# Rows of the decays' running sums spread over the partitions: TensorE products replaced by a DRAM scratch and broadcast loads, in the state-space stage of a hybrid decoder block

## The chip, the cores and the metric

The kernel runs on one NeuronCore of one Trainium2 chip. The metric is the device time of one execution in microseconds; a kernel's time is the median of several executions.

## The reference, cut to what matters

One decoder block on 1024 tokens of width 1024, all in f32: a mixer with two groups of heads (a Mamba-2 state-space group with 8 heads of 64, and a latent attention group), then a mixture of 32 experts. The change is in the state-space group, in chunks of 128 tokens:

```python
    adt = jnp.moveaxis((dt * a).reshape(b, nc, SSD_CHUNK, g, r), 2, -1)
    ...
    a_cs = jnp.cumsum(adt, axis=-1)
    decay = jnp.exp(segsum(adt))     # exp(a_cs[l] - a_cs[s]) for s <= l, else 0
    cb = jnp.einsum('bclgn,bcsgn->bcgls', cc, bc)
    y_diag = jnp.einsum('bcgrls,bcsgrp->bclgrp', cb[:, :, :, None] * decay, xd)
    decay_states = jnp.exp(a_cs[..., -1:] - a_cs)
    states = jnp.einsum('bclgn,bcgrl,bclgrp->bcgrpn', bc, decay_states, xd)
    ...
    y_off = jnp.einsum('bclgn,bcgrpn,bcgrl->bclgrp', cc, prev, jnp.exp(a_cs))
```

For each chunk and head, `decay` is a matrix of 128 x 128. With the source token `s` on the partitions, its argument needs `a_cs[s]`, one number a partition, and `a_cs[l]`, a row of 128 numbers that every partition must hold. That row is what the change is about.

## The kernel before, in words

The program is five blocks, one after the other; at the end of a block all engines meet at a barrier. Block 1 (from L294) makes the conditioning and the input projection, block 2 (L729) the attention, block 3 (L1035) the state-space stage, block 4 (L1287) the output projection and the router, block 5 (L1593) the experts. Inside a block each engine (TensorE or PE, ScalarE or ACT, VectorE or DVE, GpSimd or POOL, and SP, which here only issues DMAs) runs its own list of instructions in the order in which it is written, and waits on semaphores for the others.

Block 3 loops over `NT` = 8 chunks of `P` = 128 tokens. With `H` = 8 heads in `G` = 2 groups, `HG` = 4 heads a group. Ahead of the loop DVE works out `dt_all` and `adt` (L1159 to L1173; in the profile such small tiles are all called `slim`), PE makes `acs` and `tot`, the running sums and totals of all chunks and heads as a [128 x 64] tile each (L1045, L1046), and DVE copies them to SBUF. SP issues one load of 4 MB, `w_out_sb` (L1038), which block 4 reads.

The loop is software-pipelined: on PE and DVE `front(ch + 1)` comes before `back(ch)`.

- PE, `front`: transposes of x (L1058) and B (L1063), the product C B (L1068), and the products of L1076: for each head, `adt` of this head, broadcast over 128 columns, against the triangle `tri`. Its result is the row `a_cs[l]` on every partition, in PSUM banks 3 and 4, one for each group.
- DVE, `front`: `xd` = x dt (L1190), `cb` = C B masked (L1193), then for each group `decay` = row - `acs` (L1198) and its minimum with 0 (L1200), `xsk` (L1201), and, when ACT has taken the exponential (L1138), `decay` times `cb` (L1207).
- PE, `back`: the part from the state (L1087), the new state (L1094), the part inside the chunk (L1103, with `decay` as weights). DVE, `back`: `state` (L1216), `y_part` (L1225, L1227).
- POOL: `xds` (L1251) of the next chunk, `state_d` (L1260), `y_part` + `xsk` (L1265), gating by `zs` (L1267), and from the third chunk on two small steps of an inverse root (L361, L363).

DVE's `xd` of chunk ch waits for `ssd_ysum`, POOL's L1265 of chunk ch - 2. PE's L1058 waits for `ssd_xsk`, DVE's L1201. PE's L1076 waits for `ssd_arg`, DVE's L1200, which frees the banks, and DVE's L1198 waits for PE's L1076:

```python
                    for g in range(G):
                        if ch:
                            pe.wait_ge(S["ssd_arg"], 2 * ch - 1 + g)
                        for j in range(HG):
                            h = g * HG + j
                            last = pe.matmul(BANK[3 + g][:, j * P:(j + 1) * P], adt[:, ch, h:h + 1].to_broadcast([P, P]),
                                             tri[:, :], start=True, stop=True)
                        last.then_inc(S["ssd_rows"], 1)
```

## Time and profile before

| | |
|---|---|
| median of 3 runs | 1243.04 us (1242.4 to 1243.77) |
| the profiled execution, its own time | 1242.94 us |
| its span, first to last instruction | 1240.3 us |
| state-space stage, in the timeline | 516.39 to 603.37 us |
| PE busy | 1061.1 us, 86% of the span |
| DVE busy | 506.4 us, 41% |
| POOL busy | 210.0 us, 17% |

The durations come from that one profiled execution. A time in the timeline is counted from the start of the span. "L1198" is line 1198 of the kernel before; an f32 product is two matmul instructions in the trace, a transpose is one. Where DVE instructions don't wait, the next one starts about 0.08 us before the end of the last that the trace shows.

### The profile page before, as it was taken

The numbers are of one execution on the slowest core, as the hardware profiler recorded it, in microseconds if no ns is written. First come the engines' busy times: TensorE is split into PE (matmuls) and PEld (weight loads), VectorE is DVE, ScalarE is ACT, GpSimd is POOL, SyncE is SP. The second block draws the span as 40 slices with busy tenths as digits, with TensorE's granted clock in tenths as the row PEclk, the third lists the DMA queues.
The fourth block names the chain that finished last, engine by engine and source line by source line (L and its number), as shares of the span: only waits on it lengthen the run. The fifth ranks groups of instructions, "written<-read, shape, count | busy, mean of one in ns | idle before, by whom it ended". The sixth has DMA issues, their size and how long they took to land. (4 is left out here: it accounts for less than half of the span.)

```text
span 1240.3 us, 11686 instructions
## 1 busy us (share of the span) xinstructions
PE 1061.1 (86%) x4040; PEld 591.2 (48%) x4040; DVE 506.4 (41%) x825; ACT 260.0 (21%) x585; POOL 210.0 (17%) x324
## 2 busy tenths in 40 slices
PE   1499999996989999787699994399999999999954
PEld 1444444443455666587345553244445445444521
DVE  4543437345656555588143345511121112112217
ACT  1420001213444344233022211011111111111113
POOL 5100000223200000046210000112221221222114
PEclk9989999997999999898699996599999999999977
DMA  9763332000000000300401216238887878988537
GB/s 334 260 261 136 136 136 42 1 1 0 1 1 1 1 1 1 135 2 1 141 35 68 68 51 241 107 131 344 305 313 307 319 302 322 348 323 320 211 135 290
DMA packets 46355, 190.05 MB, mean 153 GB/s; under 512 B 17314, under 2 KB 18402, under 8 KB 29026
## 3 DMA queue, kind: packets, MB, share of 16 engines
q1 hardware_dynamic: 34596, 166.80, 35.8%
q0 software_dynamic: 10672, 18.45, 4.2%
q10 hardware_dynamic: 1040, 4.19, 0.9%
q8 instruction: 27, 0.44, 0.1%
q14 instruction: 20, 0.16, 0.0%
HBM read 182.07 MB, written 26.21 MB: 168 GB/s over the span
## 5 line engine op out<-in xcount | busy, mean ns | idle before, releaser
L1715 PE MATMUL PS<-w_gu,xg_T 128*128 128x512 f32 x544 | 241.5, 597 | 1.1 <-ACT xg_T L1800 1.1
L1715 PEld LDWEIGHTS PS<-w_gu,xg_T 128*128 128x128 f32 x544 | 101.8, 192 | 116.8 <-issue 115.2
L1726 PE MATMUL PS<-w_dn,hid_T 128*128 128x512 f32 x272 | 122.5, 593 | 0.9 <-DVE hid_T L1878 0.9
L1344 PE MATMUL PS<-w_out_sb,cat_T 128*128 128x512 f32 x256 | 113.5, 602 | 2.8 <-ACT cat_T L1400 2.8
L673 PE MATMUL PS<-hT,w_in_sb 128*128 128x512 f32 x256 | 112.2, 601 | 0.0
L1875 DVE TENSOR_TENSOR hid<-PS,hid_s 128x256 f32<-128x256 f32 x34 | 14.4, 425 | 224.2 <-ACT hid_s L1803 224.2
L361 POOL TENSOR_SCALAR rstd<-stat 128x1 f32<-128x1 f32 (+1 forms) x48 | 21.9, 456 | 408.1 <-ACT junk L468 206.3
L991 PE MATMUL PS<-kT,qT 96*128 96x512 f32 (+4 forms) x192 | 76.6, 509 | 3.0 <-ACT qT L782 3.0
L673 PEld LDWEIGHTS PS<-hT,w_in_sb 128*128 128x128 f32 x256 | 49.4, 193 | 62.1 <-issue 62.1
L1344 PEld LDWEIGHTS PS<-w_out_sb,cat_T 128*128 128x128 f32 x256 | 48.7, 193 | 62.0 <-issue 58.4
L876 DVE TENSOR_REDUCE row_max<-PS 128x1 f32<-128x1024 f32 (+7 forms) x64 | 48.2, 754 | 63.8 <-PE PS L993 63.7
L1726 PEld LDWEIGHTS PS<-w_dn,hid_T 128*128 128x128 f32 x272 | 49.2, 190 | 50.3 <-issue 49.3
L794 ACT ACTIVATE probs<-PS,row_max 128x1024 f32<-128x1024 f32 (+7 forms) x64 | 47.5, 742 | 97.8 <-DVE row_max L876 97.4
L1881 DVE COPY y_e<-PS 128x512 f32<-128x512 f32 x34 | 23.5, 692 | 95.6 <-PE PS L1726 95.6
L1803 ACT ACTIVATE hid_s<-PS 128x256 f32<-128x256 f32 x34 | 13.1, 385 | 222.5 <-PE PS L1715 222.5
L683 PE MATMUL PS<-w_in_sb,hT 128*128 128x512 f32 x128 | 56.2, 592 | 0.0
L1003 PE MATMUL PS<-ident,probs 128*128 128x128 f32 x288 | 43.4, 278 | 12.4 <-ACT probsT L802 6.9
L1657 POOL COPY dst_now<-dst_i 128x1 int32 (+1 forms) x34 | 6.2, 183 | 248.7 <-DVE y_e L1881 149.2
L1710 PEld LDWEIGHTS PS<-ident,x_g 128*128 128x128 f32 x272 | 35.9, 190 | 23.8 <-issue 15.9
L692 PE MATMUL PS<-w_in_sb,hT 128*128 128x424 f32 x128 | 46.9, 519 | 0.0
L635 PE MATMUL PS<-ident,xn 128*128 128x128 f32 x64 | 14.5, 404 | 36.7 <-DVE xn L490 36.7
L1003 PEld LDWEIGHTS PS<-ident,probs 128*128 128x128 f32 x288 | 30.9, 141 | 29.4 <-ACT probs L794 24.1
(318 smaller groups left out, 1441.1 us busy)
## 6 DMA issues: line engine op xcount, KB each, us to landing
w_gu<-in_w_gate_dram SPq DMA_DIRECT2D x34, 1024.0 KB, 4.9
w_gu<-in_w_up_dram SPq DMA_DIRECT2D x34, 1024.0 KB, 7.5
w_dn<-in_w_down_dram SPq DMA_DIRECT2D x34, 1024.0 KB, 10.6
ada_later<-in_ada_w_dram SPq DMA_DIRECT2D x16, 1024.0 KB, 4.9
ada_first<-in_ada_w_dram SPq DMA_DIRECT2D x8, 1024.0 KB, 12.6
y_g<-y_rows SPq DMA_DIRECT2D x8, 1024.0 KB, 11.8
x_in<-in_x_dram SPq DMA_DIRECT2D x8, 512.0 KB, 3.7
w_in_sb<-in_w_in_dram ACTq DMA_DIRECT2D x1, 4096.0 KB, 13.2
```

The costliest lines, as they stand in the source:

```text
L673: last = pe.matmul(BANK[4 + n % 4][:, :], w_in_sb[:, k, XC0 + ct * P:XC0 + (ct + 1) * P], hT[:, k, hh * HALF:(hh + 1) * HALF], start=(k == ...
L683: last = pe.matmul(BANK[t % 2][:, 0:IN_SSD], hT[:, k, t * P:(t + 1) * P], w_in_sb[:, k, 0:IN_SSD], start=(k == 0), stop=(k == KC - 1))
L692: last = pe.matmul(BANK[6 + t % 2][:, 0:REST], hT[:, k, t * P:(t + 1) * P], w_in_sb[:, k, XC1:], start=(k == 0), stop=(k == KC - 1))
L794: act.activation(probs[b][:, 0:n], PS[:, 2 * b:2 * b + 2, :].rearrange("p a n -> p (a n)")[:, 0:n], ACT.Exp, bias=row_max[:, b:b + 1], acc ...
L876: dve.tensor_reduce(row_max[:, b:b + 1], PS[:, 2 * b:2 * b + 2, :].rearrange("p a n -> p (a n)")[:, 0:n], AX_X, ALU.max, negate=True).then ...
L991: pe.matmul(BANK[2 * b + c0 // HALF][:, 0:c1 - c0], qT[h][0:depth(h), i * P:(i + 1) * P], kT[h][0:depth(h), c0:c1], start=True, stop=c1 < ...
L1003: last = pe.transpose(BANK[4 + j // 4][:, j % 4 * P:(j % 4 + 1) * P], probs[g % 2][:, j * P:(j + 1) * P], ident[:, :])
L1344: last = pe.matmul(BANK[2 + t % 2 * 2 + j], cat_T[t % 2][:, k, :], w_out_sb[:, k, j * HALF:(j + 1) * HALF], start=(k == 0), stop=(k == KC ...
L1710: last = pe.transpose(BANK[k // 4][:, k % 4 * P:(k % 4 + 1) * P], x_g[u][:, k::KC], ident[:, :])
L1715: last = pe.matmul(BANK[bank], xg_T[b][:, k, :], w_gu[r][:, :, k, :], start=(k == 0), stop=(k == KC - 1))
L1726: last = pe.matmul(BANK[5 + j], hid_T[b][:, k, :], w_dn[r][:, k, j * HALF:(j + 1) * HALF], start=(k == 0), stop=(k == FC - 1))
L1881: return dve.tensor_copy(y_e[b][:, HALF:], BANK[6])
```

## The change

The running sums of all chunks and heads are made a second time, transposed, by one product (`adt` as weights, `tri` moving): a [64 x 128] tile, one row for each chunk and head. DVE copies it to `acs_T`, SP stores it to a DRAM tensor `acs_rows`, and loads from it, for each chunk, the 8 rows of 128 numbers on all 128 partitions at once: 4 KB a partition, 512 KB a load, into one of four tiles `rows_b`. Four loads are issued ahead of `w_out_sb`, four behind it. The products of L1076 are gone, and `decay`'s subtraction reads `rows_b` instead of PSUM.

```diff
+        acs_T = place("acs_T", R_S + 8192, [NH, P])
+        acs_rows = nc.dram_tensor("acs_rows", [NT, H * P], F32).ap()
+        rows_b = [place(f"rows_b{i}", o, [P, H * P]) for i, o in enumerate((R_U, R_U + 4096, R_U + 8192, R_S + 4096))]
...
             @block.sync
             def _(sp):
+                def load_rows(ch):
+                    if ch >= 4:
+                        sp.wait_ge(S["ssd_arg"], 2 * (ch - 3))
+                    sp.dma_start(rows_b[ch % 4][:, :], acs_rows[ch, :].partition_broadcast(P)).then_inc(S[f"rows_in{ch % 4}"], 16)
+
+                sp.wait_ge(S["acsT_read"], 1)
+                sp.dma_start(acs_rows.rearrange("t (h l) -> (t h) l", l=P), acs_T[:, :]).then_inc(S["acs_stored"], 16)
+                sp.wait_ge(S["acs_stored"], 16)
+                for ch in range(4):
+                    load_rows(ch)
                 sp.dma_start(w_out_sb[:, :, :], w_out[0].rearrange("(p k) n -> p k n", k=KC)).then_inc(S["w_out_loaded"], 16)
+                for ch in range(4, NT):
+                    load_rows(ch)
...
                 adt_f = adt[:, :, :].rearrange("p t h -> p (t h)")
+                pe.matmul(BANK[2][0:NH, 0:P], adt_f, tri[:, :], start=True, stop=True).then_inc(S["acsT_done"], 1)
                 pe.matmul(BANK[0][:, 0:NH], tri[:, :], adt_f, start=True, stop=True)
                 pe.matmul(BANK[1][:, 0:NH], ones[:, :], adt_f, start=True, stop=True).then_inc(S["cums_done"], 1)
                 pe.wait_ge(S["cums_read"], 2)
+                pe.wait_ge(S["acsT_read"], 1)
...
                     last.then_inc(S["ssd_cb"], 1)
-                    for g in range(G):
-                        if ch:
-                            pe.wait_ge(S["ssd_arg"], 2 * ch - 1 + g)
-                        for j in range(HG):
-                            h = g * HG + j
-                            last = pe.matmul(BANK[3 + g][:, j * P:(j + 1) * P], adt[:, ch, h:h + 1].to_broadcast([P, P]),
-                                             tri[:, :], start=True, stop=True)
-                        last.then_inc(S["ssd_rows"], 1)
...
+                dve.wait_ge(S["acsT_done"], 1)
+                dve.tensor_copy(acs_T[:, :], BANK[2][0:NH, 0:P]).then_inc(S["acsT_read"], 1)
                 dve.wait_ge(S["cums_done"], 1)
...
                     for g in range(G):
                         d = decay[ch % 2 * 2 + g][:, :]
-                        dve.wait_ge(S["ssd_rows"], 2 * ch + g + 1)
-                        link(dve.tensor_tensor(d.rearrange("p (h l) -> p h l", l=P), BANK[3 + g].rearrange("p (h l) -> p h l", l=P),
+                        if g == 0:
+                            dve.wait_ge(S[f"rows_in{ch % 4}"], 16 * (ch // 4 + 1))
+                        if ch >= 2:
+                            dve.wait_ge(S["ssd_diag"], ch - 1)
+                        link(dve.tensor_tensor(d.rearrange("p (h l) -> p h l", l=P),
+                                               rows_b[ch % 4][:, g * HG * P:(g + 1) * HG * P].rearrange("p (h l) -> p h l", l=P),
                                                by_head(acs[:, ch, g * HG:(g + 1) * HG], P), ALU.subtract))
                         dve.tensor_scalar(d, d, 0.0, None, ALU.min).then_inc(S["ssd_arg"], 1)
```

The order of SP's DMAs in this block, before:

```order
L1036 UNCONDITIONAL_BRANCH [waits barrier_Pool_Activation_PE_DVE_SP_release]
L1038 DMA w_out_sb<-in_w_out_dram 128x8192
L1035 UNCONDITIONAL_BRANCH
L1289 UNCONDITIONAL_BRANCH [waits barrier_Pool_Activation_PE_DVE_SP_release]
L1294 DMA x_res_201<-in_x_dram 128x1024
```

and now, with the line numbers of the changed kernel:

```order
L1049 DMA acs_rows<-acs_T 64x128 [waits acsT_read]
L1046 DMA rows_b_200<-acs_rows 128x1024 [waits acs_stored]
L1046 DMA rows_b_201<-acs_rows 128x1024
L1046 DMA rows_b_202<-acs_rows 128x1024
L1046 DMA rows_b_203<-acs_rows 128x1024
L1053 DMA w_out_sb<-in_w_out_dram 128x8192
L1046 DMA rows_b_200<-acs_rows 128x1024 [waits ssd_arg]
L1046 DMA rows_b_201<-acs_rows 128x1024 [waits ssd_arg]
L1046 DMA rows_b_202<-acs_rows 128x1024 [waits ssd_arg]
L1046 DMA rows_b_203<-acs_rows 128x1024 [waits ssd_arg]
```

`w_out_sb` was the first thing that SP did in the block; it now stands behind two waits (for the copy and for the store) and five DMAs.

DVE's order from the running sums to the middle of chunk 0, before (`slim_193` is `adt`, `slim_194` is `acs`):

```order
L1173 SCALAR_TENSOR_TENSOR slim_193<-slim_192,a_row 128x64 [waits a_exp,dve_step]
L1177 COPY slim_194<-PS 128x64 [waits cums_done]
L1178 COPY slim_195<-PS 128x64
L1180 TENSOR_TENSOR slim_197<-slim_195,slim_194 128x64 [waits cums_read]
L1190 TENSOR_TENSOR xd_167<-PS,slim_192 128x512 [waits ssd_xT,cums_exp]
L1193 TENSOR_TENSOR cb_183<-PS,tri 128x256 [waits ssd_cb]
L1198 TENSOR_TENSOR decay_173<-PS,slim_194 128x512 [waits ssd_rows]
L1200 TENSOR_SCALAR decay_173<-decay_173 128x512 [waits dve_step]
L1198 TENSOR_TENSOR decay_174<-PS,slim_194 128x512 [waits ssd_rows]
```

and now:

```order
L1184 SCALAR_TENSOR_TENSOR slim_193<-slim_192,a_row 128x64 [waits a_exp,dve_step]
L1188 COPY acs_T<-PS 64x128 [waits acsT_done]
L1190 COPY slim_194<-PS 128x64 [waits cums_done]
L1191 COPY slim_195<-PS 128x64
L1193 TENSOR_TENSOR slim_197<-slim_195,slim_194 128x64 [waits cums_read]
L1203 TENSOR_TENSOR xd_167<-PS,slim_192 128x512 [waits ssd_xT,cums_exp]
L1206 TENSOR_TENSOR cb_183<-PS,tri 128x256 [waits ssd_cb]
L1214 TENSOR_TENSOR decay_173<-rows_b_200,slim_194 128x512 [waits rows_in0]
L1217 TENSOR_SCALAR decay_173<-decay_173 128x512 [waits dve_step]
L1214 TENSOR_TENSOR decay_174<-rows_b_200,slim_194 128x512
```

One copy is new, and the subtraction's input and its wait have changed from PSUM and PE to `rows_b` and a DMA.

## Rows read from the trace of the kernel before

**Rows 1.** The page: busy time of each engine, its share of the span, instructions.
```profile
PE 1061.1 (86%) x4040; PEld 591.2 (48%) x4040; DVE 506.4 (41%) x825; ACT 260.0 (21%) x585; POOL 210.0 (17%) x324
```

**Rows 2.** Timeline behind the stage: start, duration, what, [idle before <- releaser].
```profile
603.42 0.49 DVE L1440 TENSOR_SCALAR cat<-zs,rstd 128x512 f32<-128x512 f32 x1 [6.32 <-PEq L1035]
```

**Rows 3.** Timeline of one steady period, DVE and POOL.
```profile
565.11 0.69 DVE L1190 TENSOR_TENSOR xd<-PS,slim 128x512 f32<-128x512 f32 x1 [1.47 <-POOL y_part L1265]
...
567.11 0.68 DVE L1198 TENSOR_TENSOR decay<-PS,slim 128x512 f32<-128x512 f32 x1
...
567.39 1.04 POOL L1251 TENSOR_TENSOR xds<-xd,slim 128x512 f32<-128x512 f32 x1
567.82 0.90 DVE L1200 TENSOR_SCALAR decay<-decay 128x512 f32<-128x512 f32 x1
568.39 1.22 POOL L1260 TENSOR_TENSOR state_d<-state,slim 128x512 f32<-128x512 f32 x1
...
569.24 1.53 DVE L1207 TENSOR_TENSOR decay<-decay,cb 128x512 f32<-128x512 f32 x2
...
574.17 0.69 DVE L1190 TENSOR_TENSOR xd<-PS,slim 128x512 f32<-128x512 f32 x1 [1.48 <-POOL y_part L1265]
```

**Rows 4.** Timeline of PE: parts of two periods, and the end of the stage.
```profile
560.40 1.09 PE L1058 MATMUL PS<-ident,xbc 128*128 128x128 f32 x4 [1.99 <-DVE xsk L1201]
...
562.56 2.22 PE L1076 MATMUL PS<-tri,slim 128*128 128x128 f32 x16
...
571.18 3.00 PE L1076 MATMUL PS<-tri,slim 128*128 128x128 f32 x16
...
590.95 2.05 PE L1087 MATMUL PS<-state,xbc 128*128 128x256 f32 x4 [5.36 <-DVE y_part L1227]
...
592.79 3.51 PE L1103 MATMUL PS<-xd,decay 128*128 128x64 f32 x16
```

**Rows 5.** Waits of the stage, 522 to 600 us: total us, times, longest.
```profile
DVE decay L1198 <- PE PS L1076: 0.9, 2, 0.7
```

**Rows 6.** Timeline, start of the stage and chunk 1.
```profile
521.27 0.69 PE L1045 MATMUL PS<-slim,tri 128*128 128x64 f32 x2 [5.88 <-DVE slim L1173]
...
526.38 0.69 DVE L1198 TENSOR_TENSOR decay<-PS,slim 128x512 f32<-128x512 f32 x1 [0.69 <-PE PS L1076]
...
531.08 1.04 POOL L1251 TENSOR_TENSOR xds<-xd,slim 128x512 f32<-128x512 f32 x1 [5.13 <-DVE xd L1190]
...
531.57 0.69 DVE L1198 TENSOR_TENSOR decay<-PS,slim 128x512 f32<-128x512 f32 x1 [0.24 <-PE PS L1076]
```

**Rows 7.** DMAs, issue to landing: two medians; h_rows' stores, then x_res' loads.
```profile
c_col<-in_c_dram SPq DMA_DIRECT2D x1, 4.0 KB, 1.6
G<-in_post_norm_mix_dram POOLq DMA_DIRECT2D x1, 512.0 KB, 14.0
...
DMA to landing us min/median/max: 2.6/8.3/9.5
...
DMA to landing us min/median/max: 3.4/4.1/4.4
```

**Rows 8.** One line's instructions, the whole stage: ns min/median/max.
```profile
L1198 DVE TENSOR_TENSOR decay<-PS,slim x16: 677/681/691, 526.4 to 585.2; 128x512 f32<-128x512 f32 x16
L1207 DVE TENSOR_TENSOR decay<-decay,cb x16: 676/680/927, 529.1 to 588.2; 128x512 f32<-128x512 f32 x16
```

**Rows 9.** Timeline of chunk 2, without L361 and L363 on POOL.
```profile
538.21 1.28 POOL L1267 TENSOR_TENSOR zs<-y_part,zs 128x512 f32<-128x512 f32 x1
538.27 0.69 DVE L1190 TENSOR_TENSOR xd<-PS,slim 128x512 f32<-128x512 f32 x1 [1.48 <-POOL y_part L1265]
...
539.92 0.85 DVE L1200 TENSOR_SCALAR decay<-decay 128x512 f32<-128x512 f32 x1
...
540.44 1.24 POOL L1260 TENSOR_TENSOR state_d<-state,slim 128x512 f32<-128x512 f32 x1
...
542.48 1.28 DVE L1207 TENSOR_TENSOR decay<-decay,cb 128x512 f32<-128x512 f32 x2
```

More of the change, by code:

```diff
@@ L272, in hybrid_block @@
             kpeT_done kpe_act kpe_dve kpe_copied pad_zeroed qpe_done qpeT_done qpe_act qpe_dve v_done v_read
-            qk_done max_done exp_done pT_done pT_dve pT_act pv_done inv_done o_copied oT_done o_read dt_pos dt_exp a_exp adt_done cums_done cums_read cums_exp ssd_xT ssd_bT ssd_cb ssd_rows
+            qk_done max_done exp_done pT_done pT_dve pT_act pv_done inv_done o_copied oT_done o_read dt_pos dt_exp a_exp adt_done acsT_done acsT_read acs_stored rows_in0 rows_in1 rows_in2 rows_in3 cums_done cums_read cums_exp ssd_xT ssd_bT ssd_cb
             ssd_diag ssd_off ssd_state ssd_cbm ssd_arg ssd_xd ssd_xsk ssd_m ssd_y1 ssd_prev ssd_b ssd_exp
@@ L1174, in _ @@
                                          ALU.mult, ALU.mult).then_inc(S["adt_done"], 1)
+                flat = lambda t: t[:, :, :].rearrange("p t h -> p (t h)")
+                dve.wait_ge(S["acsT_done"], 1)
+                dve.tensor_copy(acs_T[:, :], BANK[2][0:NH, 0:P]).then_inc(S["acsT_read"], 1)
                 dve.wait_ge(S["cums_done"], 1)
-                flat = lambda t: t[:, :, :].rearrange("p t h -> p (t h)")
                 dve.tensor_copy(flat(acs), BANK[0][:, 0:NH]).then_inc(S["cums_read"], 1)
```

## The prediction

> **What bounds the kernel now.** First the page: TensorE (PE) is busy 86% of a span of 1240.3 us [rows 1]. A change that takes 128 matmul instructions off PE looks good by that line. But the share is a mean over stages, so the next view is the timeline of the state-space stage alone, 516.4 to 603.4 us. The stage ends at a barrier: VectorE (DVE) is idle for 6.32 us until it lets it go at 603.42 [rows 2]. What lengthens or shortens this stage moves everything behind it by as much. The chain that ended last, as the page prints it, lies in the expert stage and says nothing on this one.
>
> Inside the stage one chunk takes 9.06 us in the steady part (chunk products `xd` start at 565.11 and 574.17), and the rows of one such period [rows 3] show the loop: no row of DVE between them has an idle time, and the next `xd` waits 1.48 us for POOL's L1265, which itself waits for DVE's L1227. So the loop is DVE and one POOL addition. PE is not in it: it starts each front only after waiting for DVE's L1201 (1.99 us idle at 560.40), and its rows' products (L1076, from 571.18, 3.00 us) run while DVE is busy with L1225 and L1227 [rows 4]. The list of waits closes it: over the whole stage DVE waited for L1076 twice, 0.9 us together [rows 5]. That is 0.69 us in chunk 0 and 0.24 us in chunk 1 [rows 6].
>
> **The change, part by part.**
>
> *Removed: eight products per chunk on PE.* 16 matmul instructions for each of 8 chunks, 2.22 to 3.00 us a chunk in the rows shown [rows 4], are worth nothing but the 0.9 us above; the cover is DVE's own chain. With the products gone the PE work between L1227 and the next L1201 gets 2 to 3 us more slack. With longer gaps PE may be granted less clock, and it still fits: in its slowest rows the front is 2.16 us from L1058 to the start of L1076, and the back 1.84 us for L1087, as much for the equally shaped L1094, and 3.51 us for L1103 [rows 4], 9.35 us together. That is 0.3 us over today's period and under the period that I forecast below. I cost it at nothing.
>
> *Added at the start: product, copy, store, load.* `adt` is ready when PE starts at 521.27 [rows 6]. Then: the new [64 x 128] product, 0.75 us (L1045 with 64 columns took 0.69); DVE's copy of 128 columns out of PSUM, 0.3 (my estimate from 0.69 for 512); SP's wake-up, 0.1; the store of 32 KB into the scratch; a wake-up, 0.1; the load of the first 512 KB. No small store is in the trace. Its bounds are the 4 KB load of `c_col`, 1.6 us, and the quickest 512 KB store of `h_rows`, 2.6 us [rows 7]; I take 2.1, in between, since 32 KB is far from both. The load has the size of `x_res`, 3.4 to 4.4 us with median 4.1 [rows 7]; I take 4.0. So chunk 0 gets its rows at 521.27 + 0.75 + 0.3 + 0.1 + 2.1 + 0.1 + 4.0 = 528.6, where DVE's L1198 now starts at 526.38 [rows 6]: **+2.2 us** (with all the low ends +0.8, with all the high ends +3.3). Everything in the stage is behind that instruction in DVE's order, so the delay goes through to the barrier. The later products of `cums` slip by about half a microsecond, under this wait. The Trainium skill ("DMA: Bandwidth & Descriptors", section on the anatomy of one DMA) fits a transfer as 2.0 us plus bytes over 436 GB/s; by it store and load would be 2.1 and 3.2 us, and the sum 0.8 us smaller.
>
> *Moved: w_out.* Its 4 MB were issued at the stage's start; now they are behind the store and four loads on SP, so issued near 526. Their reader starts after the barrier at 603.42 [rows 2], 77 us later, while 512 KB took 4.1 us [rows 7], so 4 MB at that rate 33. That costs nothing, unless the stage shrank to half. The loads for chunks 4 to 7 wait for `ssd_arg` of the chunk four before; that leaves more than three periods (27 us) for a transfer of 4.
>
> *Changed: where L1198 reads.* This is the term that the diff hides. L1198 read PSUM and one SBUF tile; now both its inputs are in SBUF, like those of L1207. In the trace L1198 took 677 to 691 ns in all 16 cases, whatever POOL did: at 567.11 POOL's L1251 ran beside it [rows 3, 8]. L1207 took 680 ns alone, but 927 ns where it started at 569.24 under POOL's L1260, which ended at 569.61 [rows 3, 8]: overlap 0.37, lengthening 0.25. L1200 does the same, though it has one input: at 567.82 under L1251 (end 568.43), overlap 0.61, and it took 0.90 us instead of 0.43 (0.43 is its time with POOL idle), 0.47 more. So such a DVE instruction stands until POOL's is over, less about 0.12 us of its own start. The Trainium skill ("SBUF — State Buffer", section "Who interferes with whom") has the rule: a VectorE instruction with two SBUF inputs, or in a two-port mode, and a GpSimd one that reads SBUF exclude each other for a whole instruction. The row of L1207 agrees, and this rule speaks against the change.
>
> What it costs by chunk, laying the rows of POOL and DVE against each other from `xd` at 0:
> - Chunk 0: `xd` is done before the wait for the rows, so POOL's L1251 is over when they land. Nothing.
> - Chunk 1: L1198 could start 0.93 after `xd`, as in a steady period, at about 531.25; L1251 runs 531.08 to 532.12 [rows 6]. It ends at 531.25 + 0.68 + 0.75 = 532.68 instead of 532.25. **+0.4** (the 0.24 us of PE's wait is already taken off).
> - Chunks 2 and 3 (538.27 is such a period [rows 9]): POOL's L1267 lasts to 1.22, so the first L1198 ends at 1.77. L1251 comes behind it, until about 2.5; L1200 waits for that and ends at 2.8; L1260 goes next, until 3.75, and the second L1198 waits and ends at 4.3. Then L1200 0.35, L1201 0.60 (the step from one 512-column instruction to the next, as for L1207: 1.28 - 0.68), L1207 twice 1.28: end at 6.56, against 543.76 - 538.27 = 5.49 now. **+1.1 each**, 2.2.
> - Chunks 4 to 7, where POOL has L361 and L363 in between: the first L1198 takes 0.15 longer; the second L1198 gets in before L1251, which then ends at 3.7 and holds L1200 until 4.0; L1260 ends near 4.95 and holds the first L1207 for 0.3. End at 6.1 against 5.66. **+0.45 each**, 1.8.
>
> **Sum:** 2.2 + 0.4 + 2.2 + 1.8 = 6.6 us. The profiled execution took 1242.94 us, so 1249.5; the median of the runs shown is 1243.04, 0.1 above, so **1249.6 us**, 0.5% slower. About 0.2%, 2.5 us, is what a measurement of this kernel can tell from no change.
>
> **Rivals.**
> - *DVE and POOL fully take turns.* If an instruction of POOL holds out DVE for its whole length and neither slips in during the other's start, L1251 and L1260 (1.04 + 1.22 us) lie end to end with DVE's: chunks 2 and 3 end L1207 at 7.2 (+1.7), chunks 4 to 7 at 6.65 (+1.0), in all 0.4 + 3.4 + 4.0 = 7.8 instead of 4.4: 1253.0 us. The rule of the Trainium skill ("SBUF — State Buffer", the section above), taken to the letter, is this rival. Against it: L1260 started at 540.44 while L1200 was still at work until 540.77, and took 1.24 us instead of 1.22 [rows 9].
> - *Not slower: no new contention.* If the broadcast operand (`acs`, 4 numbers a partition for 512 outputs) doesn't count as a second stream, L1198 stays at 0.68 us beside POOL. Then only 2.2 - 0.24 remains: 1245.0 us, and 1243.6 with a fast pair of transfers, within 0.2%. It decides from the point where L1198's maximum is under 0.7 us. For it: the trace has no instruction of just this form. Against it: L1207's second operand (`cb`, one tile of 128 columns for four heads) is also a broadcast one, and did wait.
> - *Faster* would need PE's 0.9 us of waits back and rows that land before 526.4; two transfers in series don't fit between 522.3 and 526.4 by any row (1.6 + 3.4 is the least). It could come only from somewhere that the trace does not show.
> - *The same row read 128 times is slow.* Every partition reads the same 4 KB. The loads of `G` are such ones, and took 14.0 us, but on POOL's queue and with the DMA engines full of other work [rows 7]. If the first load took this, the start would be 10 us later: 1259.6 us.
>
> **How the numbers follow.** Forecast as summed 0.54; full turns 0.17; no contention 0.14; slow broadcast 0.07; PE late at its lower clock, or something unseen on the slow side, 0.05; faster 0.03. The range takes the forecast's own ends (0.8 to 3.3 at the start, 1.3 to 4.4 and more of contention), full turns with the high end, and reaches into the no-contention case: 1244.6 to 1255.0 us. Faster by over 0.2%: 0.03. Within 0.2%, below 1245.5: no contention and the lowest corner of the forecast, 0.17. Slower: 0.80.
>
> **What the profile after would show.** Right: DVE idle before the first decay subtraction until a DMA, which lets it go near 528.6; the subtraction's maximum well over 0.9 us, median over 0.68; periods near 10.2 us for chunks 2 and 3 and 9.5 for 4 to 7; DVE's wait for POOL's L1265 unchanged at 1.5. PE busy in the stage down by 18 to 24 us and nothing gained from it. Wrong: a subtraction flat at 0.68 (then the second rival), periods of 10 us throughout (the first), a first load of 6 us or more (the fourth), or DVE waiting for the products of L1103 in mid-stage (PE late).

## The result, and the profile after

The changed kernel takes **1249.47 us** (median of 5 runs, 1247.71 to 1250.86) against 1243.31 us for the kernel before, timed beside it: a ratio of 1.0049, 95% interval 1.0034 to 1.0064. It is slower by half a per cent. The prediction was 1249.6. The profiled execution took 1248.88 us (1242.94 before), with a span of 1246.6.

The changed lines have other numbers now: L1045 is L1063 (the new product is L1062), L1058 is L1077, L1068 (the product C B) is L1087, L1087 is L1098, L1103 is L1114, L1190 is L1203, L1198 is L1214, L1200 is L1217, L1201 is L1218, L1207 is L1224, L1251 is L1268, L1260 is L1277, L1265 and L1267 are L1282 and L1284, L361 and L363 are L366 and L368, L1440 is L1457. Beside [rows 1] stand these two lines of the page of after, busy us, share and instructions by engine:

```profile
span 1246.6 us, 11451 instructions
...
PE 1060.6 (85%) x3914; PEld 586.6 (47%) x3914; DVE 511.0 (41%) x826; ACT 260.1 (21%) x585; POOL 214.3 (17%) x324
```

126 recorded matmul instructions fewer, and 6.3 us more span. VectorE (DVE) and GpSimd (POOL) are busy longer, though POOL's program is untouched: that is the first sign of where the time went. The timeline of the stage's start, against [rows 6] (start, duration, engine, operation, and in brackets the idle time before it and what ended it):

```profile
520.96 0.69 PE L1062 MATMUL PS<-tri,slim 128*64 128x128 f32 x2 [5.88 <-DVE slim L1184]
...
521.68 0.28 DVE L1188 COPY acs_T<-PS 64x128 f32<-64x128 f32 x1 [0.78 <-PE PS L1062]
...
522.00 0.52 SPq L1049 DMA_DIRECT2D acs_rows<-acs_T  x1
...
523.83 1.77 SPq L1046 DMA_DIRECT2D rows_b<-acs_rows  x4
...
528.21 0.69 DVE L1214 TENSOR_TENSOR decay<-rows_b,slim 128x512 f32<-128x512 f32 x1 [2.21 <-DMA rows_b<-acs_rows]
...
531.17 1.09 PE L1077 MATMUL PS<-ident,xbc 128*128 128x128 f32 x4 [5.64 <-DVE xsk L1218]
...
533.07 1.04 POOL L1268 TENSOR_TENSOR xds<-xd,slim 128x512 f32<-128x512 f32 x1 [6.82 <-DVE xd L1203]
...
533.58 0.42 DVE L1206 TENSOR_TENSOR cb<-PS,tri 128x256 f32<-128x256 f32 x1 [0.59 <-PE PS L1087]
...
533.92 0.73 DVE L1214 TENSOR_TENSOR decay<-rows_b,slim 128x512 f32<-128x512 f32 x1
```

The start reads as the working had it: product to copy 0.72 us, copy 0.28, store issued at 522.00 and the loads at 523.83, first subtraction at 528.21, 7.25 us after the first product (5.11 before). And the two DVE lines that changed, each with its minimum, median and maximum in ns, against [rows 8]:

```profile
L1214 DVE TENSOR_TENSOR decay<-rows_b,slim x16: 683/778/1528, 528.2 to 591.5; 128x512 f32<-128x512 f32 x16
...
L1224 DVE TENSOR_TENSOR decay<-decay,cb x16: 678/683/926, 530.9 to 594.8; 128x512 f32<-128x512 f32 x16
```

The subtraction was flat from 677 to 691 ns; now it goes up to 1528. One period of chunk 3, DVE and POOL from two answers of the timeline (each in order of time), against [rows 9]:

```profile
550.71 0.69 DVE L1203 TENSOR_TENSOR xd<-PS,slim 128x512 f32<-128x512 f32 x1 [1.48 <-POOL y_part L1282]
...
551.65 0.82 DVE L1214 TENSOR_TENSOR decay<-rows_b,slim 128x512 f32<-128x512 f32 x1
552.50 1.15 DVE L1217 TENSOR_SCALAR decay<-decay 128x512 f32<-128x512 f32 x1
553.58 1.53 DVE L1214 TENSOR_TENSOR decay<-rows_b,slim 128x512 f32<-128x512 f32 x1
```

```profile
550.65 1.27 POOL L1284 TENSOR_TENSOR zs<-y_part,zs 128x512 f32<-128x512 f32 x1
551.88 1.49 POOL L1268 TENSOR_TENSOR xds<-xd,slim 128x512 f32<-128x512 f32 x1
553.33 1.22 POOL L1277 TENSOR_TENSOR state_d<-state,slim 128x512 f32<-128x512 f32 x1
```

First POOL's L1284 holds the subtraction (0.82 instead of 0.68), the subtraction holds POOL's L1268 (1.49; it took 1.04 in chunk 1, above), that holds L1217 (1.15 instead of 0.43), and L1277 the second subtraction (1.53). It looks as if the two engines passed one resource to and fro, and both get longer; the experiments test that.

**Where the 6.9 us of the stage lie.** The stage is taken from its first DVE instruction (`dt_raw`) to the one behind the barrier (603.42 before, 610.01 after); each cell is a difference of starts from the timeline. "Start" is first product to first subtraction, "chunks 0, 1" from there to `xd` of chunk 2, "2, 3" and "4 to 6" the mean period, "last" from `xd` of chunk 7 to the barrier. The labels are those of the experiments below. The 4.83 to 4.84 us ahead of the first product are the same in all.

| kernel | start | chunks 0, 1 | 2, 3 | 4 to 6 | last | stage |
|---|---|---|---|---|---|---|
| before | 5.11 | 11.89 | 8.89 | 9.06 | 20.19 | 86.99 |
| after | 7.25 | 12.44 | 10.06 | 9.53 | 20.65 | 93.88 |
| e1_rows_early | 4.96 | 12.63 | 10.06 | 9.54 | 20.67 | 91.83 |
| e2_wait_only | 6.81 | 13.69 | 8.71 | 9.05 | 20.17 | 90.07 |
| e3_acs_psum | 6.72 | 12.37 | 8.89 | 9.05 | 20.18 | 89.03 |
| e4_pool_light_after | 6.70 | 12.39 | 8.53 | 8.49 | 19.61 | 86.06 |
| e5_pool_light_before | 5.09 | 11.87 | 8.34 | 8.34 | 19.46 | 82.97 |
| e6_wout_first | 11.55 | 12.44 | 10.06 | 9.54 | 20.66 | 98.21 |
| e7_fused_psum | 5.70 | 12.44 | 8.29 | 8.88 | 20.01 | 86.20 |
| e8_fused_rows | 6.96 | 11.28 | 9.48 | 9.03 | 20.16 | 89.27 |
| e9_min_then_bias | 5.40 | 11.31 | 8.70 | 8.87 | 19.99 | 85.54 |
| e10_min_then_bias_rows | 6.98 | 11.34 | 8.71 | 8.88 | 20.01 | 87.20 |
| e11_pool_writes | 6.85 | 12.39 | 8.97 | 8.74 | 19.87 | 88.09 |

After minus before: 2.14 at the start, 0.55 in chunks 0 and 1, 1.17 and 1.18 in chunks 2 and 3, 0.47, 0.47, 0.46 and 0.46 in chunks 4 to 7; 6.90 in all. The stage is the sharp measure here. What lies outside it is the same program in all kernels, and still its length (span less stage) went from 1151.87 to 1155.39 us from one profiled execution to another, and from barrier to end alone from 636.25 to 639.08 us, so totals tell a microsecond or two less well than the periods do. Two columns need care as well. Each row is one profiled execution, and "start" holds a DMA load whose time varies: with the same product, copy, store and load in front of it, it came out at 6.70 to 6.98 in six other kernels (e2, e3, e4, e8, e10, e11) and at 7.25 in this one. And "chunks 0, 1" depends on the clock that TensorE was granted there (see e2 and e7).

### The profile page after: what moved, and what is told of

Its sections match the earlier page's. It is cut to its first block and busy times, and to the rows that moved or that the text cites. A ratio compares the mean times of both kernels' runs of the same rounds, so it can differ in the third digit from the quotient of the medians.

```text
span 1246.6 us, 11451 instructions
## 1 busy us (share of the span) xinstructions
PE 1060.6 (85%) x3914; PEld 586.6 (47%) x3914; DVE 511.0 (41%) x826; ACT 260.1 (21%) x585; POOL 214.3 (17%) x324
## 5 line engine op out<-in xcount | busy, mean ns | idle before, releaser
L366 POOL TENSOR_SCALAR rstd<-stat 128x1 f32<-128x1 f32 (+1 forms) x48 | 23.1, 482 | 403.7 <-ACT junk L473 204.9
L1008 PE MATMUL PS<-ident,probs 128*128 128x128 f32 x288 | 43.4, 278 | 12.4 <-ACT probsT L807 6.9
L1268 POOL TENSOR_TENSOR xds<-xd,slim 128x512 f32<-128x512 f32 x8 | 9.2, 1151 | 207.3 <-DVE xd L1203 207.3
```

Of the source, the lines that this page charges most:

```text
L1008: last = pe.transpose(BANK[4 + j // 4][:, j % 4 * P:(j % 4 + 1) * P], probs[g % 2][:, j * P:(j + 1) * P], ident[:, :])
```

## The experiments

### Is it the second SBUF input? (e3_acs_psum)

Rows by DMA as in the change, but `acs`, the subtraction's other operand, is read from PSUM, where one more product leaves it. The wait for the transfers stays, and the second SBUF input goes.

```diff
+                pe.matmul(BANK[3][:, 0:NH], tri[:, :], adt_f, start=True, stop=True)
...
-                                               by_head(acs[:, ch, g * HG:(g + 1) * HG], P), ALU.subtract))
+                                               by_head(BANK[3][:, ch * H + g * HG:ch * H + (g + 1) * HG], P), ALU.subtract))
```

> The changed kernel, but the running sums on the partitions (acs) are made a third time into PSUM bank 3, and the subtraction takes them from there; the rows still come from SBUF. So it has one SBUF input instead of two. Theory (two SBUF inputs are what collides with POOL): the subtraction is flat at 0.68 to 0.70 us, the chunk periods return to 8.9 us (chunks 2, 3) and 9.06 us (4 to 7), the stage is 4.3 us shorter than in the changed kernel, total 1245.2 us. Rival (reading rows that a DMA wrote into SBUF is slow by itself, or the long DVE rows come from the DMAs): periods stay at 10.06 and 9.53 us, total 1249.5 us.

Measured: 1244.89 us (before 1244.46), ratio 1.0000 (0.9991 to 1.0009). One line's instructions:

```profile
L1215 DVE TENSOR_TENSOR decay<-rows_b,PS x16: 674/679/687, 526.6 to 585.9; 128x512 f32<-128x512 f32 x16
```

The subtraction is flat again and every period from chunk 2 on is that of before within 0.01 us (8.89, 9.05, last 20.18), with the rows still coming by DMA. So all the extra length of those periods, 4.2 us, comes from the second SBUF input. What stays is the start, 1.6 us, and the 0.5 of chunks 0 and 1, which therefore is not the contention's.

### Only the wait (e2_wait_only)

The reverse: products and PSUM operand stay, but DVE also waits for the loaded rows, which nothing reads.

```diff
+                        for j in range(HG):
+                            h = g * HG + j
+                            last = pe.matmul(BANK[3 + g][:, j * P:(j + 1) * P], adt[:, ch, h:h + 1].to_broadcast([P, P]),
+                                             tri[:, :], start=True, stop=True)
+                        last.then_inc(S["ssd_rows"], 1)
...
-                                               rows_b[ch % 4][:, g * HG * P:(g + 1) * HG * P].rearrange("p (h l) -> p h l", l=P),
+                                               BANK[3 + g].rearrange("p (h l) -> p h l", l=P),
```

> The changed kernel with all of its product, copy, store, loads and waits, but TensorE's products of the rows are kept and the subtraction reads PSUM as before. Theory (the start costs 2.1 us, and everything else of the loss is where the subtraction reads): the first subtraction starts 7.2 us after the first product of the stage, all periods are those of the kernel before (8.9 and 9.06 us), total 1245.5 us. Rival (the loads and w_out moving while the loop runs, or the missing TensorE work, are what lengthens the periods): with the loads alone the periods are 0.5 to 1.2 us longer too, total 1248 to 1249.5 us.

Measured: 1246.80 us, ratio 1.0019 (1.0010 to 1.0028). From chunk 3 on the periods are those of before, as expected; chunks 0 and 1 took 13.69 us instead of 11.89, which was not. TensorE's (PE's) lines of the timeline in chunk 1, with the DVE line that waits for them:

```profile
530.22 0.63 PE L1077 MATMUL PS<-ident,xbc 128*128 128x128 f32 x4 [1.95 <-DVE xsk L1227]
...
531.35 3.58 PE L1095 MATMUL PS<-tri,slim 128*128 128x128 f32 x16
...
533.35 0.69 DVE L1223 TENSOR_TENSOR decay<-PS,slim 128x512 f32<-128x512 f32 x1 [1.14 <-PE PS L1095]
```

and the same in the kernel before:

```profile
529.34 0.64 PE L1058 MATMUL PS<-ident,xbc 128*128 128x128 f32 x4 [2.10 <-DVE xsk L1201]
...
530.48 1.95 PE L1076 MATMUL PS<-tri,slim 128*128 128x128 f32 x16
```

The eight row products take 3.58 us in e2 and 1.95 in before, and DVE waits for them. The windows over just these products, e2's and then that of before (columns as explained further below; the clock is the third number from the end), show why:

```profile
531.35:534.93 3.58, 3.58 (x19) 3.58 (x18) 1.97 (x4) 0.53 (x2) 1.04 (x1) 0.52 0.97 416
...
530.48:532.43 1.95, 1.95 (x19) 1.95 (x18) 1.67 (x4) 0.14 (x1) 1.04 (x1) 1.00 0.00 0
```

The granted clock was 0.52 in e2, nearly all at 1.2 GHz, and 1.00, 2.4 GHz, in before. Why it fell there is open. It was not a longer pause of PE: ahead of chunk 1 PE was idle for 1.95 us in e2 and for 2.10 in before, and its first products came back at the higher clock in both (0.63 and 0.64 us). e7 below shows the same slow products where nothing ahead of them had changed. So the 1.8 us (of which 0.4 came back in chunk 2, 8.52 instead of 8.89) is not shown to be a cost of the wait; in the medians e2 stands 2.3 us above before, in the one profiled stage 3.1.

### Only the contention (e1_rows_early)

The rows are loaded from an input that is there from the start, so nothing waits for a store.

```diff
-                    sp.dma_start(rows_b[ch % 4][:, :], acs_rows[ch, :].partition_broadcast(P)).then_inc(S[f"rows_in{ch % 4}"], 16)
+                    sp.dma_start(rows_b[ch % 4][:, :], x[0, ch, :].partition_broadcast(P)).then_inc(S[f"rows_in{ch % 4}"], 16)
...
-                sp.wait_ge(S["acsT_read"], 1)
-                sp.dma_start(acs_rows.rearrange("t (h l) -> (t h) l", l=P), acs_T[:, :]).then_inc(S["acs_stored"], 16)
-                sp.wait_ge(S["acs_stored"], 16)
```

> The changed kernel without the store and without the wait for it: the eight loads take rows of the input x in place of the running sums, and the first four go out at the start of the stage. The decays are then those of other numbers, which leaves the instructions and their lengths as they are, but can change how many expert tiles the last block does, so the stage in the trace decides. Theory: the 2.1 us of the start are gone (first subtraction 5.1 to 5.5 us after the first product), the periods keep their 10.06 and 9.53 us, so the stage is 93.9 - 2 = 91.9 us long against 87.0 before. Rival (a late start throws POOL and DVE out of step, and the longer periods follow from it): periods back near 9 us, stage 87.5 us.

Measured: 1246.17 us, ratio 1.0012 (1.0002 to 1.0021). The start is back at 4.96 us and every later period is that of after: stage 91.83, where 91.9 was expected. So start and contention are two separate sums. The total rose by 1.7 us and the stage by 4.8. The rest lies outside the stage, which is 1151.87 us long here, the shortest of all profiled executions; the recorded matmul instructions are as many as in after (3914), so no expert tile less shows, and the cause stays open.

### POOL taken out, on both kernels (e4, e5)

POOL's products `xds` and `state_d` write one column of each head instead of all, so they take next to no time.

```diff
-                    pool.tensor_tensor(heads(xds[ch % 2][:, :]), heads(xd[ch % 2][:, :]), by_head(dec_out[:, ch, :], HD),
+                    pool.tensor_tensor(heads(xds[ch % 2][:, :])[:, :, 0:1], heads(xd[ch % 2][:, :])[:, :, 0:1], by_head(dec_out[:, ch, :], 1),
...
-                        pool.tensor_tensor(heads(state_d[:, :]), heads(state[:, :]), by_head(dec_all[:, ch, :], HD), ALU.mult)\
+                        pool.tensor_tensor(heads(state_d[:, :])[:, :, 0:1], heads(state[:, :])[:, :, 0:1], by_head(dec_all[:, ch, :], 1), ALU.mult)\
```

> The changed kernel with POOL's xds and state_d cut to one column a head (the rest is zeroed once at the start), so the state carries almost nothing; the other engines' instructions are unchanged, but values reach the router changed, so the stage in the trace decides and not the total. Theory: with POOL's 1.04 and 1.22 us gone from the middle of the chunk, the subtraction is over 0.7 us only in the first group, for POOL's zs (0.82 us), periods near 8.5 us in chunks 2 to 7, stage 93.9 - 7.3 = 86.6 us. Rival (the subtraction from SBUF is slow whatever POOL does): periods stay over 9.3 us.

> The kernel before with the same cut of POOL's xds and state_d. The stage in the trace decides. Theory: the minimum and the product with cb no longer wait, 0.54 us less in chunks 2 and 3, 0.72 in 4 to 7, periods 8.35 us, stage 87.0 - 4.0 = 83.0 us. Then the two kernels stand 3.5 us apart in place of 6.9: the start's 2.1, 0.5 for chunk 1, and 0.15 for each of six chunks. Rival (as for the run above): they stay 6.9 us apart.

Measured: e4 1241.33 us, ratio 0.9987 (0.9977 to 0.9996); e5 1239.92 us, ratio 0.9972 (0.9963 to 0.9982), against 1243.64. The stages differ by 3.1 us (86.06 and 82.97) where after and before differ by 6.9: 1.6 at the start, 0.5 in chunks 0 and 1, and 0.14 to 0.20 a chunk behind them. From chunk 2 on after and before differ by 4.2 us and these two by 1.0. So two POOL instructions a chunk make 3.2 us of the change; the other 0.5 by which the stages come closer is the quicker first load (start 6.70 instead of 7.25), which POOL has no part in. The 0.5 of chunks 0 and 1 is still there without the two POOL instructions. What is left per chunk shows in e4's subtraction:

```profile
L1214 DVE TENSOR_TENSOR decay<-rows_b,slim x16: 671/684/829, 527.4 to 584.4; 128x512 f32<-128x512 f32 x16
```

Its maximum of 829 ns is the first subtraction beside `zs` (L1284), which stayed. The kernel *before* has, as the expectation had it, 4.0 us of the same contention (86.99 to 82.97), on its minimum L1200 and on L1207.

### A POOL instruction that only writes (e11_pool_writes)

As e4, but ahead of each narrowed product POOL fills the whole tile.

```diff
+                    link(pool.memset(xds[ch % 2][:, :], 0.0))
...
+                        link(pool.memset(state_d[:, :], 0.0))
```

> The changed kernel with POOL's xds and state_d replaced by fills with zero of the same tiles, which write SBUF and read none of it (and one column a head as in the light runs); the state carries almost nothing. The stage in the trace decides. Theory (DVE's second SBUF input and POOL's reads are what exclude each other, so a writing POOL holds out no subtraction): the subtraction is over 0.70 us only in the first group, 0.82 us, for zs, and periods are near those of the light run, 8.5 us. Rival (any POOL instruction on SBUF, also a fill, holds out the subtraction): the second group's subtraction is longer by up to the fill's length, periods over 9 us.

Measured: 1244.38 us, ratio 1.0007 (0.9997 to 1.0018), stage 88.09. The timeline of one chunk:

```profile
541.18 0.82 DVE L1214 TENSOR_TENSOR decay<-rows_b,slim 128x512 f32<-128x512 f32 x1
541.39 0.53 POOL L1276 MEMSET xds<- 128x512 f32 x1
...
542.03 0.91 DVE L1217 TENSOR_SCALAR decay<-decay 128x512 f32<-128x512 f32 x1
...
542.14 0.53 POOL L1286 MEMSET state_d<- 128x512 f32 x1
```

The fill at 541.39 ran wholly beside the two-input subtraction and took its usual 0.53 us; in its place in the changed kernel, started 0.23 us after the subtraction, the product L1268 took 1.49 instead of 1.04. But the one-input minimum L1217 took 0.91 instead of 0.43 beside the second fill. The fill did not hold the subtraction either: its 0.82 us is what it takes in e4 too, behind `zs`. The subtraction is thus held by what POOL reads, the minimum also by what it writes. The Trainium skill ("SBUF — State Buffer", section "Who interferes with whom") says just this: two SBUF inputs collide only with a GpSimd instruction that reads SBUF, a two-port mode, which a one-input `tensor_scalar` can enter, with any. The run agrees on both (0.82 and 0.91 us). The periods, 8.97 and 8.74 us, were longer than the 8.5 that I had expected, by this collision on the minimum, which I had not priced.

### The order of the transfers (e6_wout_first)

The change also moved `w_out` behind the small store. Here it goes first.

```diff
+                sp.dma_start(w_out_sb[:, :, :], w_out[0].rearrange("(p k) n -> p k n", k=KC)).then_inc(S["w_out_loaded"], 16)
                 sp.wait_ge(S["acsT_read"], 1)
...
-                sp.dma_start(w_out_sb[:, :, :], w_out[0].rearrange("(p k) n -> p k n", k=KC)).then_inc(S["w_out_loaded"], 16)
```

> The changed kernel with the 4 MB load of w_out back at the head of SP's list, ahead of the store and the loads of the rows. Theory (the transfers of one queue go in order, and w_out then lies in front of the rows): the store lands at the earliest when w_out is done, 12.5 us after 516.1, the first rows near 529 + 3.5 = 532.5, so the first subtraction is 4.3 us later than in the changed kernel, total 1253.8 us. Rival (the transfers share the DMA engines fairly): store and load are each about twice as long, 4 us more or less the same by another way, but with the store landing before w_out does; if the order does not matter at all, 1249.5 us.

Measured: 1255.52 us, ratio 1.0091 (1.0074 to 1.0108). From the DMA view of this kernel (KB, then median us to landing), and its waits:

```profile
w_out_sb<-in_w_out_dram SPq DMA_DIRECT2D x1, 4096.0 KB, 12.4
...
acs_rows<-acs_T SPq DMA_DIRECT2D x1, 32.0 KB, 6.6
```

```profile
DVE decay L1214 <- DMA rows_b<-acs_rows: 6.5, 1, 6.5
```

The 32 KB store, issued at 522.89, lands 6.6 us later, at 529.5, when the 4 MB in front of it (issued at 516.98, 12.4 us) are in; in after it took 1.8. Start +4.3 us against after, all else alike. With the new placement the move of `w_out` costs nothing, and it is a needed part of the change.

### Versions without the contention (e7 to e10)

**e7_fused_psum**, on the kernel before: subtraction and minimum in one instruction per head, straight from PSUM, with `acs` as a scalar of each partition. Nothing of DVE's decay work reads SBUF as a second stream then.

```diff
-                        link(dve.tensor_tensor(d.rearrange("p (h l) -> p h l", l=P), BANK[3 + g].rearrange("p (h l) -> p h l", l=P),
-                                               by_head(acs[:, ch, g * HG:(g + 1) * HG], P), ALU.subtract))
-                        dve.tensor_scalar(d, d, 0.0, None, ALU.min).then_inc(S["ssd_arg"], 1)
+                        for j in range(HG):
+                            last = dve.tensor_scalar(d[:, j * P:(j + 1) * P], BANK[3 + g][:, j * P:(j + 1) * P],
+                                                     acs[:, ch, g * HG + j:g * HG + j + 1], 0.0, ALU.subtract, ALU.min)
```

> The kernel before (products on TensorE, rows in PSUM), with the subtraction and the minimum of each head in one instruction of 128 columns with two scalars, out of PSUM: 8 instructions a chunk instead of 4, one SBUF input less, nothing that waits for POOL. From the steps between instructions of 128 columns out of PSUM, 0.21 us, the piece from the first subtraction to xsk takes 1.7 us instead of 2.1 (POOL idle) or 2.7 (POOL busy). Theory (the loop is bound by DVE and by its turns with POOL): 0.45 us less for chunks 0 and 1, 0.9 for 2 and 3, 0.6 for 4 to 7, total 5 us less than before, 1238.2 us. Rival (something else, the exponentials on ScalarE or TensorE, becomes the bound at once): total 1242 to 1243.5 us, with DVE idle before the products with cb or the y sums.

A miss: 1243.63 us, ratio 0.9992 (0.9983 to 1.0001), where 1238.2 was expected.

```profile
L1199 DVE TENSOR_SCALAR decay<-PS,slim x64: 341/344/351, 526.4 to 584.8; 128x128 f32<-128x128 f32 x64
```

```profile
574.08 2.15 DVE L1199 TENSOR_SCALAR decay<-PS,slim 128x128 f32<-128x128 f32 x8
...
576.41 1.04 POOL L1261 TENSOR_TENSOR state_d<-state,slim 128x512 f32<-128x512 f32 x1
...
576.74 1.87 DVE L1208 TENSOR_TENSOR decay<-decay,cb 128x512 f32<-128x512 f32 x2
```

Eight such instructions take 2.15 us, a step of 0.26 from one to the next, and from the first of the four that they replace to `xsk` it is 2.13 us where POOL is idle (526.38 to 528.51 in before): a quarter of the columns does not cost a quarter of the 0.60 us between two instructions of 512. POOL's `state_d`, free of its partners, moved on against L1208 and held that (1.87 for two, 1.28 when free). Saved are 0.6 us in each of chunks 2 and 3 and 0.18 in the later ones. In the first two columns of the table 1.1 us are lost again, where DVE waits 2.1 us for PE's row products instead of 0.9 [rows 5]:

```profile
524.41 3.62 PE L1076 MATMUL PS<-tri,slim 128*128 128x128 f32 x16
```

These are chunk 0's products, 2.22 us in before. The edit is not their cause: PE's list and all its instructions up to them are those of before. They ran at 1.2 GHz throughout here, while in before the clock rose during them. So two profiled executions can differ by about a microsecond at this place by the clock alone, and the 1.1 us do not speak against the fused form.

**e8_fused_rows**: the same instructions on the changed kernel, from `rows_b`.

```diff
+                            last = dve.tensor_scalar(d[:, j * P:(j + 1) * P], rows_b[ch % 4][:, o:o + P],
+                                                     acs[:, ch, g * HG + j:g * HG + j + 1], 0.0, ALU.subtract, ALU.min)
```

> The changed kernel with subtraction and minimum fused, one instruction of 128 columns a head out of the rows in SBUF. Theory (a minimum or subtraction from SBUF without a second tensor collides with POOL too, as L1200 did, and the start stays): 4 fewer long waits but POOL's 2.3 us still stand between DVE's instructions, so it lies between the changed kernel and the fused form out of PSUM: 1245 to 1247 us, and some of the 128-column instructions are over 0.8 us. Rival (only an instruction with two SBUF tensors collides): no instruction over 0.4 us, 1240.5 us, which is the fused form out of PSUM plus the start.

Measured: 1244.08 us, ratio 1.0005 (0.9996 to 1.0015), below the 1245 to 1247 expected; stage 89.27.

```profile
L1216 DVE TENSOR_SCALAR decay<-rows_b,slim x64: 273/278/1165, 529.1 to 588.8; 128x128 f32<-128x128 f32 x64
```

Quicker alone than from PSUM (278 ns against 344), but with a maximum of 1165: with one tensor from SBUF it collides all the same.

**e9_min_then_bias**, on the kernel before: min(a - b, 0) = min(a, b) - b, so DVE takes only the minimum of PSUM row and `acs`, and ScalarE subtracts `acs` as the bias of its exponential.

```diff
-                        act.activation(d, d, ACT.Exp).then_inc(S["ssd_exp"], 1)
+                            last = act.activation(dj, dj, ACT.Exp, bias=neg_acs[:, ch, g * HG + j:g * HG + j + 1])
...
-                                               by_head(acs[:, ch, g * HG:(g + 1) * HG], P), ALU.subtract))
-                        dve.tensor_scalar(d, d, 0.0, None, ALU.min).then_inc(S["ssd_arg"], 1)
+                                          by_head(acs[:, ch, g * HG:(g + 1) * HG], P), ALU.min).then_inc(S["ssd_arg"], 1)
```

> The kernel before, with DVE taking only min(row, acs) out of PSUM (one instruction of 512 columns a group) and ScalarE taking exp(x - acs) a head, with -acs as its bias: the same decays with one DVE instruction a group in place of two, and none that waits for POOL between xd and xsk. From the steps of the trace (0.60 us a DVE instruction of 512 columns, 0.27 us a ScalarE instruction of 128): xsk starts 2.1 us after xd in place of 3.5, then the products with cb wait for the exponentials and for POOL and end at 4.6 us (chunks 2, 3) or 5.0 us (4 to 7) in place of 5.5 and 5.7. Theory (DVE's own chain and its turns with POOL bound the loop): periods 8.0 and 8.4 us, stage 87.0 - 5.1 = 81.9 us, total 5 us below before. Rival (the eight exponentials on ScalarE become the bound): DVE idle for ScalarE over 0.7 us a chunk, stage 86 us or more.

**e10_min_then_bias_rows**: the same with the rows by DMA and `acs` from PSUM, as in e3.

> The same, with the rows out of the scratch in DRAM as in the changed kernel, and acs out of PSUM so that the minimum has one SBUF input. Theory (what is left of the change when its reading from SBUF is mended is the start, some 2 us, and nothing comes back from the work taken off TensorE): stage 2 to 2.8 us longer than in the run above, 84 to 84.7 us, total 3 us below before. Rival (with a shorter DVE chain TensorE becomes the bound where it still makes the rows, so that the loads pay): stage equal to or shorter than in the run above.

Measured: e9 1241.94 us against 1243.85, ratio 0.9986 (0.9977 to 0.9995), stage 85.54, where 81.9 was expected; e10 1242.30, ratio 0.9988 (0.9979 to 0.9997), stage 87.20. e9 is a miss by 3.6 us of the 5.1. Its exponentials, and a steady chunk:

```profile
L1141 ACT ACTIVATE decay<-decay,neg_acs x64: 384/388/401, 526.2 to 585.0; 128x128 f32<-128x128 f32 x64
```

```profile
565.20 2.44 ACT L1141 ACTIVATE decay<-decay,neg_acs 128x128 f32<-128x128 f32 x8
...
566.33 1.05 POOL L1264 TENSOR_TENSOR state_d<-state,slim 128x512 f32<-128x512 f32 x1
...
566.57 1.96 DVE L1211 TENSOR_TENSOR decay<-decay,cb 128x512 f32<-128x512 f32 x2 [0.70 <-ACT decay L1141]
```

DVE gave up two instructions a chunk, but now waits for ScalarE, whose eight exponentials take 2.44 us (0.70 us in this chunk, 5.7 us in the stage), and then for POOL. The time of an exponential with such a bias is what the Trainium skill states ("ScalarE: Activation LUTs", section "What ACT_TABLE_LOAD costs"): about 280 ns plus 0.833 ns a column, 387 ns for 128, and the trace has 388; I had not used it. e9's stage is 1.45 us shorter than that of before and its total 0.14% lower. The prediction took 0.2% as what can be told from no change, and e10 shows why totals are not enough here: its total is 0.12% lower than before, also with an interval that excludes 1, while its stage is 0.2 us longer. e10's stage is 1.66 us longer than e9's (2 to 2.8 expected), all of it but 0.08 at the start: even with the contention gone, rows by DMA are no better than rows by products.

## Why the prediction was right, and where it was not

The mechanism was right in its two main parts, a chain of transfers at the start and a subtraction that takes turns with POOL. That 1249.6 and 1249.47 agree within 0.2 us is in part luck: the stage grew by 6.90 us where 6.6 were summed, the medians differ by 6.16, and the start of this one profiled execution was the longest of seven with the same transfers.

- **What bounds the stage: right.** The loop of DVE and POOL is what got longer; the wait of `xd` for L1282 is still 1.48 us (chunk 3, above).
- **Start: right, +2.14 us against +2.2**, with two small errors that cancel. The store landed in 1.8 us, not 2.1, and from the load's issue to the subtraction it took 4.38, not 4.1 with its wake-up. The load's time varies: 3.8 us in e3, 4.0 in e11, so the start cost 1.6 to 1.9 us in the other kernels. The two ends given for it, +0.8 and +3.3, don't follow from their rows: with 1.6 and 3.4 us for the transfers it is +1.1, with 2.6 and 4.4 it is +3.1. The Trainium skill's figures ("DMA: Bandwidth & Descriptors", the section on the anatomy of one DMA) gave 0.8 us less; that fit is for transfers that GpSimd issues, and these are SP's. The measured store (1.8) is 0.3 us under it and the load (3.8 to 4.4) 0.6 to 1.2 us over it, near the rows of this kernel's own `x_res`.
- **w_out: right**, nothing; e6 shows what the old place would have cost, which the prediction did not ask. One term in it was mis-sized: the first load behind `w_out`, issued at 530.45 for chunk 4, took 14.1 us to land and not 4. Its rows were read from 561.71 on, so the 27 us of slack covered it, and the first load stayed the only one that DVE waited for:

```profile
DVE decay L1214 <- DMA rows_b<-acs_rows: 2.2, 1, 2.2
...
DMA to landing us min/median/max: 3.3/5.8/14.1
```

- **Chunk 1: right size (+0.55 against +0.4), wrong cause.** The step said that L1251 (now L1268) would hold the subtraction for 0.4 us. The subtraction took 0.73. Instead DVE waited 0.59 us for PE's L1087 before `cb`, in the first lines of the profile after: PE had been idle for 5.64 us, and L1077 took 1.09 us. In before that pause was 2.10 us and the same transposes took 0.64 (529.34, shown at e2). The windows (PE, weight loads, DVE, ACT, POOL busy, then the granted clock as a share, DMA share, GB/s) show the lower of the two clocks, 1.2 GHz, in after; the last line is the first window in before:

```profile
523.00:533.00 10.00, 4.22 (x19) 3.96 (x20) 6.06 (x12) 3.08 (x9) 1.04 (x1) 0.50 0.91 311
...
583.00:593.00 10.00, 8.60 (x32) 7.42 (x32) 8.42 (x13) 2.87 (x7) 6.60 (x7) 0.50 0.00 0
...
523.00:533.00 10.00, 7.90 (x56) 7.66 (x57) 7.42 (x15) 3.44 (x10) 2.09 (x2) 0.87 0.45 195
```

  All kernels without the row products have PE idle for 3.5 to 9.9 us there and the transposes at 1.09 us, and all but e10 have the wait of 0.59 us; and e3 (12.37) and e4 (12.39, against 11.87 in e5) have the half microsecond without the contention. Removing PE work was costed at nothing "and it still fits": true from chunk 2 on (the second window is at the lower clock too, and no DVE wait in chunks 2 to 7 is longer for it), false for the first two chunks, where the path runs through PE once.
- **PE busy down by 18 to 24 us: wrong.** The stage's matmul time went from 60.63 us to 58.77 (windows of the whole stage), though 126 of 396 instructions are gone: at a granted clock of 0.66 instead of 0.81 the rest takes longer. It was worth nothing, as said.
- **Chunks 2 and 3: right, +1.17 and +1.18 against +1.1**, and step by step: from `xd` the first subtraction ended at 1.76 us (1.77 worked out), L1217 at 2.94 (2.8), the second subtraction at 4.40 (4.3).
- **Chunks 4 to 7: right, +0.47, 0.47, 0.46, 0.46 against +0.45**: as worked out, the second subtraction slips in before L1268, and L1217 and the first L1224 pay. One such period, DVE and POOL from two timelines:

```profile
570.31 0.69 DVE L1203 TENSOR_TENSOR xd<-PS,slim 128x512 f32<-128x512 f32 x1 [1.47 <-POOL y_part L1282]
...
571.25 0.82 DVE L1214 TENSOR_TENSOR decay<-rows_b,slim 128x512 f32<-128x512 f32 x1
...
572.45 0.68 DVE L1214 TENSOR_TENSOR decay<-rows_b,slim 128x512 f32<-128x512 f32 x1
573.17 1.22 DVE L1217 TENSOR_SCALAR decay<-decay 128x512 f32<-128x512 f32 x1
...
574.91 1.53 DVE L1224 TENSOR_TENSOR decay<-decay,cb 128x512 f32<-128x512 f32 x2
```

```profile
572.24 0.86 POOL L368 TENSOR_TENSOR rstd<-rstd,minus_half 128x2 f32<-128x2 f32 x1
573.06 1.04 POOL L1268 TENSOR_TENSOR xds<-xd,slim 128x512 f32<-128x512 f32 x1
574.06 1.22 POOL L1277 TENSOR_TENSOR state_d<-state,slim 128x512 f32<-128x512 f32 x1
```

- **The argument against "full turns" was misread.** It said that L1260 started under L1200 and took 1.24 us instead of 1.22 [rows 9], so POOL was hardly held. But 1.22 is not its free time: with no DVE instruction in its way `state_d` takes 1.04 (e7) and 1.05 (e9). The 1.22 had 0.18 us of waiting in it in every chunk, and where the overlap is long POOL is held as much as DVE (1.49 against 1.04). The forecast still beat that rival, since a waiting engine does not lose its whole turn: what an instruction gains in length is, in these rows, the overlap less 0.12 to 0.15 us, on DVE and on POOL. In chunk 3 POOL's L1268 overlaps the subtraction by 0.59 us and is 0.45 longer; L1214 overlaps L1277 by 0.97 and is 0.85 longer.
- **"No new contention"** fell with the maximum of 1528 ns and with e3; **slow broadcast** with a load that served DVE after 4.38 us.

## What to carry to other kernels

Before moving an operand from PSUM to SBUF, look at what GpSimd does at that moment: the same VectorE instruction took 0.68 us from PSUM and up to 1.53 from SBUF, and the way to price it is to lay the two engines' rows side by side, each instruction waiting for the other's end. Matmuls taken off an engine that nobody waits for give nothing, and a step through DRAM (here 6.2 us from issue of the store to first use) is paid in full where it starts a chain. Take a reference duration from a row with the other engine idle, and not from the median, which may hold the waiting already.

## What was not expected of the hardware

- POOL is held by VectorE as VectorE by POOL: `xds` 1.49 us instead of 1.04, and even a POOL instruction on two columns 0.86 instead of 0.71 (L368, 572.24 above).
- A one-input VectorE instruction on 128 columns with a scalar per partition takes 344 ns out of PSUM and 278 out of SBUF; one step out of PSUM is 0.26 us, against 0.60 for the two-input instruction on 512 columns.
- A 128x512 fill by POOL (0.53 us) does not hold a two-input VectorE instruction, but does hold the one-input minimum (0.91 instead of 0.43).
- A small store behind a 4 MB load on the same queue lands when the load is through: 6.6 us instead of 1.8.
- With the row products gone PE pauses for 3.5 to 9.9 us ahead of chunk 1 and comes back at 1.2 GHz (1.09 us for transposes that took 0.64), which cost the first two chunks 0.5 us.
- The clock granted at one place differs between profiled executions with the same PE instructions up to there: chunk 0's row products took 2.22 us in before and 3.62 in e7. One trace each does not settle a difference of a microsecond at such a place.
